# Decoder layer on one core: x and B of blocks 2 to 4 turned by VectorE through DRAM instead of by TensorE

## The reference

```
proj = einsum('bld,de->ble', rms_norm(h), w_in)          # u | z | x,B,C | dt
xbc  = silu(causal_dwconv(xBC, conv_w, conv_b))           # 4 taps along tokens
cb   = einsum('bclgn,bcsgn->bclsg', C, B)                 # chunks of 128 tokens
y_diag = einsum('bclsgr,bcsgrp->bclgrp', cb * decay, x * dt)
states = einsum('bclgn,bclgr,bclgrp->bcgrpn', B, decay_to_end, x * dt)
y_off  = einsum('bclgn,bcgrpn,bclgr->bclgrp', C, prev_state, exp(a_cs))
y = rms_norm_of_group((y_diag + y_off + d_skip * x) * silu(z))
h = h + concat[pool_mixer(u), y] @ w_out ;  h = h + relu(rms_norm(h) @ w_ff1)^2 @ w_ff2
```

## Time and profile before

| | us |
|---|---|
| median of 3 runs | 2664.63 (2664.2 to 2665.22) |
| profiled execution | 2663.49 |
| its span, first to last instruction | 2661.8 |
| TensorE busy | 2642.3 (99%) |
| VectorE busy | 1661.3 (62%) |
| ScalarE busy | 1252.7 (47%) |
| GpSimd busy | 1092.2 (41%) |

### The profile page before, as it was taken

The page is one execution under the profiler, slowest core; times in us unless marked ns, Lnnn a source line. Parts: engine busy times, 40 slices in busy tenths (PEclk is TensorE's granted clock), DMA queues, the critical chain, the costliest instruction groups (busy, mean ns, idle before and its releaser), DMA issues.

```text
span 2661.8 us, 37490 instructions
## 1 busy us (share of the span) xinstructions
PE 2642.3 (99%) x13962; PEld 2213.7 (83%) x13962; DVE 1661.3 (62%) x2228; ACT 1252.7 (47%) x2526; POOL 1092.2 (41%) x866
## 2 busy tenths in 40 slices
PE   8999999999999999999999999999999999999998
PEld 6888788888888888898888888888888888888887
DVE  6788615788157882377853576564445765666667
ACT  4667653666236672256634455554545222222223
POOL 2133440335003350033443688665655535353434
PEclk9999999999999999999999999999999999999999
DMA  9977666744558536575473655673436742423323
GB/s 335 303 259 244 240 243 248 241 175 179 216 184 262 189 146 248 202 211 209 167 269 135 225 190 208 249 266 131 173 132 226 295 145 103 164 95 127 119 95 158
DMA packets 278850, 532.70 MB, mean 200 GB/s; under 512 B 63994, under 2 KB 146942, under 8 KB 270606
## 3 DMA queue, kind: packets, MB, share of 16 engines
q1 hardware_dynamic: 278670, 530.31, 56.6%
HBM read 384.31 MB, written 145.95 MB: 199 GB/s over the span
## 4 chain that ended last, share of the span: by engine, by line
PE 96%; SPq 1%; DMA 1%; DVE 1%; issue 0%; ACT 0%; POOL 0%; POOLq 0%; ACTq 0%
PE bank L2260 23%; PE bank L2228 22%; PE bank L1849 21%; PE bank L1956 13%; PE bank L1936 8%; PE bank L2040 2%; PE bank L2002 1%; PE bank L2057 1%; PE bank L2020 1%; PE bank L2028 1%; DMA w_scr<-w_both 1%; PE bank L2008 1%; SPq L730 0%; PE bank L1968 0%; PE bank L2015 0%
## 5 line engine op out<-in xcount | busy, mean ns | idle before, releaser
L1849 PE MATMUL bank<-hnT_hi,w_ring 128*128 128x512 f32 x1152 | 367.0, 391 | 0.0
L2260 PE MATMUL bank<-w_first,T_hi 128*128 128x512 f32 x896 | 275.8, 389 | 0.0
L2390 DVE SCALAR_TENSOR_TENSOR acc<-pre,par,acc 128x512 f32<-128x512 f32 x240 | 211.4, 881 | 82.6 <-ACT pre L1365 76.8
L1849 PEld LDWEIGHTS bank<-hnT_hi,w_ring 128*128 128x128 f32 x1152 | 216.2, 188 | 44.7 <-ACT win_tmp L1494 0.5
L2756 DVE TENSOR_TENSOR acc_th<-bank,acc_th 128x512 f32<-128x512 f32 x224 | 150.0, 685 | 157.5 <-PE bank L2260 156.6
L2228 PE MATMUL bank<-T_hi,w_both 128*128 128x512 f32 x768 | 242.5, 389 | 0.5 <-DVE ff L2697 0.5
L1956 PE MATMUL bank<-w_ring,T_hi 128*128 128x512 f32 x768 | 239.0, 392 | 0.0
L1849 PE MATMUL bank<-hnT_lo,w_ring 128*128 128x512 f32 x576 | 224.4, 390 | 0.0
L2260 PEld LDWEIGHTS bank<-w_first,T_hi 128*128 128x128 f32 x896 | 168.2, 188 | 34.9
L1936 PE MATMUL bank<-w_ring,hnT_hi 128*128 128x384 f32 x768 | 195.8, 335 | 1.3 <-DMA w_ring<-w_scr 1.3
L1849 PE MATMUL bank<-hnT_hi,w_both 128*128 128x512 f32 x544 | 182.0, 406 | 0.9 <-ACT pre L1365 0.9
(11 more groups left out here) (316 smaller groups left out, 6255.4 us busy)
## 6 DMA issues: line engine op xcount, KB each, us to landing
w_ring<-w_scr SPq DMA_DIRECT2D x312, 512.0 KB, 4.3
T_scr<-stage SPq DMA_DIRECT2D x32, 1792.0 KB, 6.7
w_scr<-w_both SPq DMA_DIRECT2D x100, 512.0 KB, 4.2
pair_raw<-in_w_ff SPq DMA_DIRECT2D x36, 1024.0 KB, 5.5
third<-T_scr SPq DMA_DIRECT2D x28, 1024.0 KB, 4.9
pair_raw<-T_scr SPq DMA_DIRECT2D x28, 1024.0 KB, 4.8
sums<-sums_scr SPq DMA_DIRECT2D x64, 384.0 KB, 4.9
raw<-in_w_in SPq DMA_DIRECT2D x36, 512.0 KB, 6.5
```

Of the source, the lines that this page charges most:

```text
L1849: mm = nc.tensor.matmul(bank[s][:, :], w[:, k, :], t[:, k, :], start=(k == 0 and j == 0), stop=(k == KT - 1 and j == 2))
L2260: mm = nc.tensor.matmul(bank[4 * half + t][:, :], a[:, k, tok], w[:, k, :], start=(SECOND[q % 7] not in GOES_ON and k == 0 and j == 0), st ...
L2390: ins = nc.vector.scalar_tensor_tensor(acc[:, s, 0:TB], pre[:, s, k:k + TB], w, acc[:, s, 0:TB], ALU.mult, ALU.add)
```

## The change

In blocks 2 to 4 `slot1` has no transposes and bank 4 or 5 isn't used for them. Instead `finish` of items 0, 2, 3 and 4 is two linked VectorE operations: the last operation of the convolution writes back to pre (for B still to F), and a 32 x 32 square transpose writes F (for B the tile b_turn, which is win_tmp). ScalarE issues a store of the tile to DRAM (256 KB) behind `evac` of the item after next. SyncE loads chunk by chunk, four DMAs of 32 x 16 x 32 elements each (64 KB in runs of 128 bytes), which put the squares in their places in xt, tokens on the partitions. The loads of group g-1 stand in SyncE's queue at j = 0 of group g (chunks 0 and 1, and chunk 3 of the group before that), at j = 4 (chunk 2), and in the down projection for the last group. b_turn shares its memory with the rows of the decays (acsT) and with the pooling's scratch, so VectorE waits for b_stored and sums_stored, and ScalarE's write of acsT for b_stored. ScalarE's copy of x out of the bank goes; B's high part is read from xt. The sixteen stores of the turned h move from SyncE's queue to ScalarE's: four behind item 6, four behind item 7, four behind item 8, four at the end of step 0. Block 1 keeps TensorE's transposes, with one copy of bank to xt in place of two.

```diff
+                def load_tokens(b, g, c):
+                    xt_stored.wait(sp, b, 48 * (g + 1))
+                    b_stored.wait(sp, b, 16 * (g + 1))
+                    if b or g:
+                        b0, q0 = (b, (g - 1) * CH + c) if g else (b - 1, STEPS - CH + c)
+                        xw_ready.wait(sp, b0, q0 + 1)
+                        ty_ready.wait(sp, b0, q0 + 1)
...
+                    for j in range(4):
+                        sp.dma_start(xt[32 * j:32 * j + 32, c, :].rearrange("p (k f) -> p k f", f=32),
+                                     blocks[j]).then_inc(xt_loaded[c].sem, 16)
...
+                        if b and g and j == 0:
+                            if g > 1:
+                                load_tokens(b, g - 2, 3)
+                            load_tokens(b, g - 1, 0)
+                            load_tokens(b, g - 1, 1)
+                        if b and g and j == 4:
+                            load_tokens(b, g - 1, 2)
...
-                        if b and n == 16:
-                            for t in range(CH):
-                                store_turned_h(b - 1, t)
...
+                            if b and d == 0 and i < 2:
+                                load_tokens(b, GROUPS - 1, 2 + i)
...
+                def store_turned(b, v):
+                    n = unit_of(b, v) if b and v >= 0 else None
+                    if n is None or n >= U_POOL or n % UNITS_G not in (0, 2, 3, 4):
+                        return
+                    g, j = divmod(n, UNITS_G)
+                    act.dma_start(xt_scr[b, g, j - 2 if j else 3], turn_tile(g, j)
+                                  ).then_inc(xt_stored.sem if j else b_stored.sem, 16)
...
                     up_out.wait(act, b, v - 1)
+                    evacuate(b, v, s, ps)
+                    store_turned(b, v - 2)
...
+                            if b:
+                                b_stored.wait(act, b, 16)
                             nc.scalar.activation(acsT, bank[3][0:HEADS, :], ACT.Copy
                                                  ).then_inc(acsT_ready.sem, 1)
+                        if b and n >= 6:
+                            store_turned_h(b - 1, n - 6)
...
-                        nc.scalar.activation(b_both[q % 2][:, 0, :] if b else b_plain[:, q % 2, :],
-                                             bank[4 + q % 2][:, GW:GW + P], ACT.Copy)
-                        nc.scalar.activation(xb[:, :], bank[4 + q % 2][:, 0:GW], ACT.Copy
-                                             ).then_inc(xb_ready.sem, 1)
+                            nc.scalar.activation(b_both[q % 2][:, 0, :], xt[:, c, GW:GW + P],
+                                                 ACT.Copy).then_inc(b_hi_ready.sem, 1)
...
+                        if b and q == 0:
+                            store_turned_h(b - 1, CH - 1)
...
-                    for i, j in enumerate((2, 3, 4, 0)):
-                        mm = nc.tensor.transpose(bank[4 + q % 2][:, i * P:(i + 1) * P],
-                                                 group_tile(g, j)[:, cols], ident[:, :])
...
+                        dst = group_tile(g, 0) if j == 0 else pre[:, s, 0:TB]
+                        steps.link(nc.vector.scalar_tensor_tensor(dst, pre[:, s, 0:TB], 1.0,
+                                                                  acc[:, s, 0:TB], ALU.add,
+                                                                  ALU.mult))
+                        if j == 0 and g:
+                            b_stored.wait(dve, b, 16 * g)
+                            sums_stored.wait(dve, b, 16 * GROUPS)
+                        nc.vector.transpose(turn_tile(g, j), dst).then_inc(up_out.sem, 1)
```

More of the change, by code:

```diff
@@ L453, in dt_bank, with x_tokens @@
             return bank[2] if b else bank[3]
+        def x_tokens(eng, b, q):
+            if b:
+                xt_loaded[q % CH].wait(eng, b, 64 * (q // CH + 1))
+            else:
+                xb_ready.wait(eng, b, q + 1)
         def m_stage(j):
@@ L753, in _ @@
                     meta_pair(j)
-                initial = [s for s in signals if s.start and s not in (state_ready, ffn_loaded, *sums_loaded)]
+                initial = [s for s in signals if s.start and s not in (state_ready, ffn_loaded, xb_ps, xb_ready, b_hi_ready,
+                                                             *sums_loaded)]
                 for j in range(4, POOL_PAIR):
```

102 lines of the change are left out of this document (68 added, 34 removed).

## The result

| | before | after |
|---|---|---|
| median, us | 2664.41 (2663.35 to 2665.22, 4 runs) | 2681.74 (2679.78 to 2683.38, 4 runs) |
| profiled execution | 2663.49 | 2680.78 |
| its span | 2661.8 | 2679.1 |
| TensorE busy | 2642.3 | 2639.0 |
| VectorE busy | 1661.3 | 1670.0 |

The ratio is 1.0065 with a 95% interval of 1.0048 to 1.0082: slower by 17.3 us. The forecast was 2682 in a range of 2664 to 2710. The median came out where it was forecast by luck: two of the terms that gave it were wrong, and their errors cancel.

The account below looks back on a forecast made before the run. TensorE was taken as the bound, VectorE as hidden second bound of groups 0 to 2. Per block 3.0 + 3.0 + 1.4 - 1.2 = +6.2 us, three blocks +18.6, giving about 2682; range 2664 to 2710.

Parts of the forecast that it names:

- TensorE's saving: Blocks 2 to 4: four transposes dropped in each of 48 steps, 0.49 us each step, 23.5 us in all.
- Price of a transposed finish: VectorE's turned finish costs 0.70 us over a plain one: 0.58 for the transpose, 0.12 for the link.
- Groups 1 and 2: VectorE's yo comes 1.57 us later, so TensorE's state product starts 0.7 later per group, +1.4 per block.
- rival 2: VectorE is not late because GpSimd's operations move clear of its own; faster, about 2645 us; chance 0.10.
- Rival 2's deciding point: TensorE keeps its saving if yo of q = 6 comes 1.1 us earlier, GpSimd's moving giving back 2.7 per group.
- Decays: Start of a block: turned items 2, 3 and 4 make TensorE wait 1.4 us before the decays' transposes.
- Block starts: Up to the state product of q = 2: 3.0 us behind ScalarE's stores plus 3.0 for DMA transfers, per block.
- contention: Block start: stores and loads of x meet the weight burst, 15 us added where 6 fit; 3 us per block.
- ScalarE's fours: Block start: each four of h's stores holds ScalarE for 3.8 us, 0.94 an issue.
- Rival 1: ScalarE's queue starves as 128-byte packets alternate with 4 KB weight rows; second four over 8 us; about 2708; chance 0.22.
- Last group: Steps q = 12 to 15: y_norm's chain lets TensorE use 0.30 of 0.49 us saved per step, -1.2 per block.

Follow-up runs that it names:

- run 1: Changed kernel with h's sixteen stores back on SyncE at n = 16, behind the loads of x there; 2699.05 us.
- run 12: Changed kernel with h's stores on ScalarE moved to the quiet steps q = 1, 2, 3 and 5, SyncE's order unchanged; 2663.72 us.
- run 3: Changed kernel with the decay sums' store ahead of the first loads of x on SyncE, h's stores left on ScalarE; 2695.14 us.
- run 2: Kernel before with only h's stores moved to ScalarE, x and B still turned by TensorE; 2708.60 us.
- run 4: Changed kernel with h's stores on SyncE behind the loads of x, and the decay sums' store ahead of those loads; 2695.78 us.
- run 5: Changed kernel with h's sixteen stores on SyncE at n = 16, ahead of the loads of x there; 2688.02 us.
- run 6: Changed kernel with h's stores on SyncE at n = 16 ahead of the loads of x, and the decay sums' store before the first loads; 2683.37 us.
- run 8: Kernel before with one GpSimd operation of 128 x 1 put in ahead of the low part of the state; one execution, 2669.02 us.
- run 10: Kernel before with h's stores on ScalarE in the quiet steps q = 1, 2, 3 and 5; 2664.20 us.

## Why the prediction was right, and where it was not

That 2682 was met within 0.3 us is luck. Term by term:

- **TensorE's saving** (48 x 0.49 = 23.5 us): mis-sized. It is 0.40 a step, 19 us, since the next product is 0.1 longer without the transposes ahead of it.
- **Price of a transposed finish** (0.70, with 0.58 for the transpose and 0.12 for the link): right, 0.72 to 0.75.
- **Groups 1 and 2** (+0.7 each): wrong in sign, -1.4 each. The waits of 1.5 to 3 us before the state product didn't come. The step that failed is that four finishes come and nothing else changes in VectorE's chain. yo was to come 1.57 later from the diagonal and came 0.68 earlier. That is the mechanism of rival 2, which I gave 0.10 and argued away: GpSimd's moving was to give back 2.7 us per group to decide it, and I held that its product with x wouldn't move. It was enough that the meetings changed order. The 3.5 us by which operations of q = 5 and q = 6 had been slowed went (two third taps, 0.7 and 0.8, xdt and xw of both steps, 1.0 each; those of q = 4 stayed slow), and 1.3 came back on two finishes. With 2.9 for four finishes and the 1.23 of gaps that makes -0.5, against -0.7 measured. Rival 2's deciding point was nearly reached: TensorE keeps 1.3 to 1.5 us a group of the 1.6 that can be had.
- **Decays** (1.4): 0 in block 2, 0.95 in blocks 3 and 4; a little high.
- **Block starts** (+6.0): +9.3 on average. I had 3 us for "contention" and priced it as transfers that don't fit. What the transfers did instead was delay one unit's weights that TensorE needed at once, and a wait of 4 us made it run at half clock for another 5. In block 4 the fours also made it wait 3.9 us for the low part of the state. Runs 1 and 12 show that h's stores on ScalarE are most of all this. My sum had no term for the clock at all. I wrote that TensorE needs only one of the three units of the burst at once; it was just that one which was late.
- **ScalarE's fours** (3.8 us each, 0.94 an issue): this size was carried from SyncE's row, where it is a mean over sixteen, and no four on ScalarE has it: measured 2.8, 4.7, 9.1 and 5.7 in block 3, and 0.46 an issue in a quiet step.
- **Rival 1**: right in mechanism; the test I named for it, "the second four lasts over 8 us", looked one four too early. The third did in block 3 (9.1 us; 3.4 and 7.4 in blocks 2 and 4). In the change as made it was partly escaped, by the table under run 3. Alone, in the kernel before (run 2), it gives 2708.6. I had written about 2708, but for the whole change, so that the two numbers meet is chance.
- **Last group** (-1.2): -1.0 to -1.1, right. y_norm bounds it, with 0.05 us of slack where there was 0.29.

The errors per block, +3.3 and -4.3, cancelled. From the waits the sum closes to 1.3 us: new waits 21.7, half clock 8.5, seven items beside short waits that last 0.2 longer 1.2, less 19.2 of saving, plus 2.7 of it that the last groups (y_norm, 0.13 a step) and VectorE (0.2 a group) take back, gives 14.9; measured 16.2. The other 1.3 I leave open: it isn't idle time of TensorE, whose gaps under 0.1 us come to 0.1 us in both kernels.

## What to carry to other kernels

When stores of short runs move to another engine's queue, look first at what the DMA engines carry at that time: beside a burst of 3 to 4 KB rows their queue slowed to less than a sixth (162 packets per us instead of 1070), the queue fills, and the issue itself holds the engine. The same stores some 25 to 55 us later in the block cost nothing. Before moving a DMA within a queue, write down for each transfer behind it when it is needed; four of these runs (1, 4, 5 and 6) were lost to a load that was wanted sooner than what stood ahead of it.

## What the runs showed of the hardware

- Who is held at the port that VectorE and GpSimd share is settled by starts 0.04 to 0.12 us apart, and it is worth 0.5 to 0.8 us per meeting. One GpSimd operation of 0.19 us put in ahead took 1.1 us off a VectorE chain of 38.4 (run 8); in the changed kernel such meetings gave 2.2 us net, against 2.9 for the four transposed finishes. A chain that has such meetings can't be summed from the old durations alone.
- A 32 x 32 square transpose of 128 x 512 by VectorE takes 0.71 us in the records and 0.63 to 0.64 from start to start.
- After TensorE stood still for 3.8 us its granted clock was 0.50 for 5 us, so the pause cost 6.3 us in all.
- The issue of one store of h (1024 runs of 128 bytes) took ScalarE 0.31 to 0.71 us in the quiet steps (run 10, all 48) and up to 10.2 us in the weight burst (run 2).
